# Query rows of the latent layer: 32x32 blocks turned on VectorE and carried by GpSimd in place of transposes on TensorE

## The reference, cut to what matters

```python
u = rms_norm(h, ln) @ w_in                       # -> c_q (512), c_kv (512), k_pe (64), gate (2048)
q = (rms_norm(c_q, ln_q) @ w_q_up).reshape(B, S, 16, 192)
kv = (rms_norm(c_kv, ln_kv) @ w_kv_up).reshape(B, S, 16, 256)
v = kv[..., 128:]
k = concatenate([kv[..., :128], broadcast(k_pe)], axis=-1)
q = rms_norm(q, g_q); k = rms_norm(k, g_k)
q = concatenate([q[..., :128], rope(q[..., 128:], pos)], axis=-1)
k = concatenate([k[..., :128], rope(k[..., 128:], pos)], axis=-1)
o = causal_dense_attention(q, k, v)
return h + (o * silu(gate)) @ w_o
```

## Time and profile before

| | before |
|---|---|
| median of 3 runs | 1396.17 us (1396.0 to 1396.33) |
| profiled execution | 1396.6 us, its span 1394.8 us |
| TensorE busy (matmul) | 1389.4 us |
| VectorE busy | 1040.2 us |
| ScalarE busy | 782.6 us |
| GpSimd busy | 101.5 us |
| granted TensorE clock | 1.00 throughout |

### The profile page before, as it was taken

The page is one execution under the profiler, slowest core; times in us unless marked ns, Lnnn a source line. Parts: engine busy times, 40 slices in busy tenths (PEclk is TensorE's granted clock), DMA queues, the critical chain, the costliest instruction groups (busy, mean ns, idle before and its releaser), DMA issues.

```text
span 1394.8 us, 17859 instructions
## 1 busy us (share of the span) xinstructions
PE 1389.4 (100%) x6584; PEld 1162.1 (83%) x6584; DVE 1040.2 (75%) x1825; ACT 782.6 (56%) x1288; POOL 101.5 (7%) x67
## 2 busy tenths in 40 slices
PE   9999999999999999999999999999999999999999
PEld 6888888888888888888888888888888888888887
DVE  6767767847667868778877886887888688779753
ACT  6577877756544654464465465446545545644642
POOL 0101001000010001010101100101010010001000
PEclk9999999999999999999999999999999999999999
DMA  9653544455556545655654654564556456555554
GB/s 357 228 180 126 163 141 149 148 189 176 184 187 208 184 157 179 206 166 170 192 182 151 208 185 151 191 201 156 176 183 205 155 185 194 163 182 186 167 179 149
DMA packets 71223, 252.40 MB, mean 181 GB/s; under 512 B 7904, under 2 KB 8288, under 8 KB 71136
## 3 DMA queue, kind: packets, MB, share of 16 engines
q1 hardware_dynamic: 70704, 249.95, 54.9%
q10 hardware_dynamic: 432, 1.31, 0.3%
HBM read 249.14 MB, written 2.10 MB: 180 GB/s over the span
## 4 chain that ended last, share of the span: by engine, by line
PE 98%; DMA 1%; DVE 0%; ACT 0%; SPq 0%; POOL 0%; issue 0%
PE acc L1317 90%; PE turn L1349 1%; PE pv_bank L1581 1%; PE score L1566 1%; PE score L1561 1%; PE pv_bank L1585 1%; PE pv_bank L1361 1%; PE score L1457 1%; PE score L1459 1%; DMA raw<-in_w_in 1%; PE og_bank L1369 0%; PE turn L1443 0%; PE pv_bank L1446 0%; PE og_bank L1446 0%; POOL rms L434 0%; PE pv_bank L1340 0%
## 5 line engine op out<-in xcount | busy, mean ns | idle before, releaser
L837 DVE TENSOR_TENSOR w_lo<-raw,w_hi 128x1024 fp32r<-128x1024 f32 x463 | 571.4, 1249 | 196.6 <-ACT w_hi L486 192.7
L486 ACT ACTIVATE w_hi<-raw 128x1024 fp32r<-128x1024 f32 x463 | 482.2, 1050 | 364.0 <-PE acc L1317 355.7
L1317 PE MATMUL acc<-w_hi,xa_hi 128*128 128x512 f32 x956 | 378.6, 396 | 0.3 <-DVE w_lo L837 0.2
L1317 PE MATMUL acc<-w_hi,xa_lo 128*128 128x512 f32 x956 | 373.1, 390 | 0.0
L1317 PE MATMUL acc<-w_lo,xa_hi 128*128 128x512 f32 x956 | 372.5, 390 | 0.0
L1317 PE MATMUL acc<-w_hi,xb_hi 128*128 128x512 f32 (+1 forms) x640 | 249.5, 390 | 0.0
L1317 PE MATMUL acc<-w_hi,xb_lo 128*128 128x512 f32 (+1 forms) x640 | 245.9, 384 | 0.0
L1317 PE MATMUL acc<-w_lo,xb_hi 128*128 128x512 f32 (+1 forms) x640 | 245.6, 384 | 0.0
L1317 PEld LDWEIGHTS acc<-w_hi,xa_lo 128*128 128x128 f32 x956 | 179.4, 188 | 37.9
L1317 PEld LDWEIGHTS acc<-w_hi,xa_hi 128*128 128x128 f32 x956 | 179.7, 188 | 37.4 <-issue 1.1
L1317 PEld LDWEIGHTS acc<-w_lo,xa_hi 128*128 128x128 f32 x956 | 179.7, 188 | 35.6
(11 more groups left out here) (179 smaller groups left out, 1143.9 us busy)
## 6 DMA issues: line engine op xcount, KB each, us to landing
raw<-in_w_b SPq DMA_DIRECT2D x320, 512.0 KB, 3.8
raw<-in_w_out_a SPq DMA_DIRECT2D x32, 512.0 KB, 3.3
raw<-in_w_out_b SPq DMA_DIRECT2D x32, 512.0 KB, 3.3
raw<-in_w_gate SPq DMA_DIRECT2D x30, 512.0 KB, 3.6
raw<-in_w_kv SPq DMA_DIRECT2D x16, 512.0 KB, 3.9
raw<-in_w_in SPq DMA_DIRECT2D x15, 512.0 KB, 6.0
raw<-in_w_q SPq DMA_DIRECT2D x16, 384.0 KB, 3.0
res<-in_x_tok SPq DMA_DIRECT2D x4, 512.0 KB, 8.0
```

The costliest lines, as they stand in the source:

```text
L486: nc.scalar.activation(w[0][:, s, 0:width], raw[:, s, 0:width], ACT.Copy).then_inc(hi_ready, 1)
L837: nc.vector.tensor_tensor(w[1][:, s, 0:width], raw[:, s, 0:width], w[0][:, s, 0:width].bitcast(F32), ALU.subtract).then_inc(lo_ready, 1)
L1317: last = nc.tensor.matmul(out, x(a), y(b), start=start and k == 0, stop=stop and k == 2, **more)
```

## The change

The unrotated query rows take the way that the keys have already: VectorE turns 32x32 blocks of `rows[:, 1]` in place (`mla_query_blocks`) in step 7, after that step's part of the attention and before its `lows`, and GpSimd carries the 16 blocks to `qT` (`query_moves`). ScalarE applies the gain in place in `qT`, in step 2 of the next pair as before, but ahead of its wait for TensorE. TensorE transposes the two rotated tiles alone. ScalarE still carries the keys; of its 16 key moves one goes from step 0 of the next pair to step 3. The last pair does the same within the output projection.

```diff
-KEY_MOVES = {3: range(0, 1), 4: range(1, 4), 7: range(4, 8), 8: range(8, 16)}
+KEY_MOVES = {3: range(0, 2), 4: range(2, 5), 7: range(5, 9), 8: range(9, 16)}
...
+        def nope_rows(buf, span):
+
+            return rows[:, buf, :, 0:2 * span].rearrange("p t (u d) -> p t u d", d=span)[:, :, :, 0:P]
...
+            def query_moves(par):
+
+                queries = nope_rows((MLA_CHAIN_0 + 1) % 2, QK)
+                turned = qT[:, par * 512:(par + 1) * 512].rearrange("p (u t d) -> p t u d", t=TILES, d=P)
+                for n in range(16):
+                    a, b = n // 4, n % 4
+                    last = nc.gpsimd.tensor_copy(turned[b * QUAD:(b + 1) * QUAD, :, :, a * QUAD:(a + 1) * QUAD],
+                                                 queries[a * QUAD:(a + 1) * QUAD, :, :, b * QUAD:(b + 1) * QUAD])
+                last.then_inc(query_turned, 1)
+
             for i in range(0, PAIRS):
-                for s in range(MLA_STEPS):
-                    if s == 1:
-                        chain(i * 2 + MLA_CHAIN_0, 2 * TILES)
-                    if s == 7:
-                        chain(i * 2 + (MLA_CHAIN_0 + 1), 2 * TILES)
+                par = i % 2
+                if i:
+                    pool.wait_ge(query_turned, i)
+                chain(i * 2 + MLA_CHAIN_0, 2 * TILES)
+                chain(i * 2 + (MLA_CHAIN_0 + 1), 2 * TILES)
+                pool.wait_ge(rms_ready, i * 2 + (MLA_CHAIN_0 + 2))
+                pool.wait_ge(query_blocks, i + 1)
+                query_moves(par)
...
-            def mla_queries_turned(par, rnd):
-
+            def mla_queries_turned(i, par, rnd):
+
+                act.wait_ge(query_turned, i)
+                at = qT[:, par * 512:(par + 1) * 512]
+                nc.scalar.activation(at, at, ACT.Copy, scale=gn("q_nope"))
                 act.wait_ge(turn_full, rnd + 1)
-                nc.scalar.activation(qT[:, par * 512:(par + 1) * 512], turn[:], ACT.Copy, scale=gn("q_nope"))
...
                     if s == 5:
+                        if i:
+                            act.wait_ge(query_turned, i)
...
+            def mla_query_blocks(i):
+
+                dve.wait_ge(rows_ready, i * 2 + (MLA_CHAIN_0 + 2))
+                queries = nope_rows((MLA_CHAIN_0 + 1) % 2, QK)
+                nc.vector.transpose(queries, queries).then_inc(query_blocks, 1)
...
                     mla_attend(i, par, s, later, fill)
+                    if s == 7:
+                        mla_query_blocks(i)
...
-            def mla_turn(c, buf, rnd, rope_bank, head_step, rope_0, heads=2):
+            def mla_turn(c, buf, rnd, rope_bank, rope_0):
 
                 pe.wait_ge(rows_ready, c + 1)
                 pe.wait_ge(turn_read, rnd)
-                for h in range(heads):
-                    for t in range(TILES):
-                        nc.tensor.transpose(turn[:, h * SEQ + t * P:h * SEQ + (t + 1) * P],
-                                            rows[:, buf, t, h * head_step:h * head_step + P], ident[:])
```

More of the change, by code:

```diff
@@ L319, in build_program @@
         key_blocks = sem("key_blocks")
+        query_blocks = sem("query_blocks")
+        query_turned = sem("query_turned")
         rot_step = sem("rot_step")
@@ L440, in _ @@
             chain(1, TILES)
-            for i in range(0, PAIRS):
-                for s in range(MLA_STEPS):
-                    if s == 1:
-                        chain(i * 2 + MLA_CHAIN_0, 2 * TILES)
-                    if s == 7:
-                        chain(i * 2 + (MLA_CHAIN_0 + 1), 2 * TILES)
+            def query_moves(par):
[6 more added lines that the diff above has]
+                last.then_inc(query_turned, 1)
+            for i in range(0, PAIRS):
+                par = i % 2
[6 more added lines that the diff above has]
+                query_moves(par)
+            pool.wait_ge(query_turned, PAIRS)
             pool.wait_ge(loaded, 48)
@@ L685, in mla_pair @@
                     if s == 2 and later:
-                        mla_queries_turned(1 - par, mla_round(i, 0))
+                        mla_queries_turned(i, 1 - par, mla_round(i, 0))
                     if s == 3:
@@ L706, in _ @@
                 if k == 4:
-                    mla_queries_turned(1, mla_round(PAIRS, 0))
+                    mla_queries_turned(PAIRS, 1, mla_round(PAIRS, 0))
                 i, _, s = after_pairs(k)
@@ L1161, in mla_pair @@
                     mla_attend(i, par, s, later, fill)
+                    if s == 7:
+                        mla_query_blocks(i)
                     if s == 2:
                         dve.wait_ge(rows_ready, i * 2 + (MLA_CHAIN_0 + 1))
-                        keys = rows[:, MLA_CHAIN_0 % 2, :, 0:2 * P]
+                        keys = nope_rows(MLA_CHAIN_0 % 2, P)
                         nc.vector.transpose(keys, keys).then_inc(key_blocks, 1)
@@ L1208, in _ @@
                     mla_query_rotate(PAIRS - 1)
+                    mla_query_blocks(PAIRS - 1)
                 if k in OUT_FILL_END:
@@ L1483, in mla_queries_turned @@
             def mla_queries_turned(i, par, rnd):
-                mla_turn((i - 1) * 2 + (MLA_CHAIN_0 + 1), (MLA_CHAIN_0 + 1) % 2, rnd, pv_bank, QK, 2 * QK)
+                mla_turn((i - 1) * 2 + (MLA_CHAIN_0 + 1), (MLA_CHAIN_0 + 1) % 2, rnd, pv_bank, 2 * QK)
             def mla_pair(i, par, later, steps=MLA_STEPS):
@@ L1506, in mla_pair @@
                     if s == 3:
-                        mla_turn(i * 2 + MLA_CHAIN_0, MLA_CHAIN_0 % 2, mla_round(i, 1) if later else 4, og_bank, P, 2 * P, 0)
+                        mla_turn(i * 2 + MLA_CHAIN_0, MLA_CHAIN_0 % 2, mla_round(i, 1) if later else 4, og_bank, 2 * P)
             latents = [tuple(x[:, c] for x in lat) for c in range(2)]
```

## The result

The changed kernel takes **1402.16 us** (median of 6 runs, 1401.84 to 1402.57) against 1396.09 us for the kernel before in the same comparison (6 runs): ratio 1.0044, 95% interval 1.0033 to 1.0054. It is 6.1 us slower. The forecast was 1393.2 us, and its chances for "faster" and "within 0.2%" held three quarters; what came is the first rival, "the moves are too slow".

A forecast was written before the change was run, and what follows sets the result against it. TensorE was taken to bound the kernel, with ScalarE's exponential chain last in pairs 2 to 7. 6 x 0.32 + 2 x 0.56 = 3.0 us less gave a 1393.2 us median; 8-in-10 range 1391.5 to 1404 us.

The forecast's parts named there:

- the moves are too slow: Rival: GpSimd's copies overrun and delay the key power and TensorE; 1399.5 us at 0.30 us a move; chance 0.35.
- What bounds the kernel now: TensorE sets the time, but in pairs 2 to 7 waits 0.30 us each for ScalarE's exponential, whose chain ends last.
- I take 0.20 us: Assumed time of one GpSimd query move, 3.2 us for a pair's sixteen, leaving 0.5 us to spare.
- The limit of 0.234 us a move: Most a GpSimd move may take before the key power is late: 3.74 us of free time for 16 moves.
- The low halves: VectorE's low halves at 196.05 to 197.25 and 197.75 to 198.7 keep GpSimd's copies out for their whole length.
- The overshoot o: Time by which GpSimd's moves run past 201.94, when the key power is wanted; sum 6 x (0.32 - o) + 1.1 us.
- The four transposes, 0.56 us a pair,: TensorE's saving from four transposes less in each pair, 4.5 us over eight pairs if TensorE alone set the time.
- The chain gives 0.32 us in pairs 2 to 7: One key move less in ScalarE's step 0 shortens the chain to the exponential by 0.32 us a pair.
- The whole 0.56 us: Full transpose saving claimed for the first turned queries (pair 1) and the last (output projection).
- The covers: Idle time or slack was to hide VectorE's 0.70 us block turn, later loads, ScalarE's 0.32 us step 3 move and gain.
- The moves shut VectorE out: Rival: sixteen GpSimd copies in a row hold the shared access and delay VectorE's low halves; 1398 us; chance 0.07.
- The chain gives way: Rival: TensorE's wait at 207.98 has more slack, so the full 4.5 us come out; 1391.7 us; chance 0.08.

The follow-up runs named there:

- e5: Changed kernel with GpSimd's key power between the twelfth move and the last four, and ScalarE copying the rotated parts ahead of the gain: 1405.92 us.
- e7: Changed kernel with VectorE's block turn of the queries behind the low half of step 7, the last pair unaltered: 1404.33 us.
- e6: Changed kernel with ScalarE copying the two rotated parts ahead of the gain, not behind it: 1401.85 us.
- e8: Changed kernel with 12 query moves on GpSimd, four on ScalarE, and the last pair's block turn one output projection step later: 1394.71 us.
- e11: Changed kernel with only the last pair's block turn one step later in the output projection: 1402.47 us.
- e9: Changed kernel with TensorE's four transposes of the query rows put back, into a bank nobody reads: 1402.45 us.
- e2: Changed kernel with GpSimd carrying only 12 or 4 of 16 query blocks, the others left out: 1395.81 us and 1394.72 us.
- e10: Changed kernel with GpSimd carrying all key blocks and ten query blocks, ScalarE six, the last block turn one step later: 1395.97 us.

## Why the prediction was wrong, step by step

- **What bounds the kernel now** held. TensorE's wait for the exponential was the place, and it took the loss of the changed kernel in pairs 2 to 7 and the small gain with 12 or 4 moves. The further losses of e5 and e7 show at the scores, behind the gain, a path that the prediction named only as a cover.
- **The step that failed is the term "I take 0.20 us" for a GpSimd move.** It was worked out from 128-partition fills, which read nothing. Measured are 0.29 us for a copy and 0.33 us from start to start, so 16 x 0.328 = 5.25 us in place of 3.2: 2.05 us more against a margin of 0.5 us. That a copy follows the one before closely held (0.04 us); what was too small is the copy itself, for which the text's lower bound had 0.115 us. The limit of 0.234 us a move was strict but fair (the runs put it at (5.89 - 0.14 - 1.50) / 16 = 0.266); the taken value had no row of a copy behind it. The nearest row in kind, ScalarE's 0.32 us for the same 32x128 block, was in the text, as an example inside the rival, and it was right. The estimate that the text made by the Trainium skill (GPSIMD Engine Reference, on performance against the Vector engine and on pitfalls), 0.28 us a move, was nearer than mine as well: the copy took 0.29, but its start to start took 0.33.
- **The low halves** were counted too dear. They took 0.83 and 0.67 us from the copies (1.12 and 0.96 less the usual 0.29), 1.50 in place of 2.15 us: each of the two copies began 0.22 and 0.13 us into its low half, and part of its own 0.29 us ran beside. With the 0.14 us between block turn and first copy the power starts 5.25 + 1.50 + 0.14 = 6.9 us after the block turn; 5.89 were free. The overshoot o is 1.0 us, and 6 x (0.32 - 1.0) = -4.1 us; measured were -3.9. The direction of the exclusion was right and its size fair.
- **The four transposes, 0.56 us a pair,** were mis-sized. Before, the six loads from 201.44 to the next `acc` at 202.21 took 0.77 us; now two take 0.34 us (204.63 to 204.97). The saving is 0.43 us. I had read it off the starts of two groups, and the first group's start-up stays with whatever group is first.
- **"The chain gives 0.32 us in pairs 2 to 7"** could only be seen with the overshoot taken away: with 12 or 4 moves the pairs are 26.76 us against 27.02 to 27.03, so 0.27 us. TensorE's wait there is 0.45 us, which is 0.30 + 0.43 - 0.27; 0.54 was forecast. So this half of the forecast was the right mechanism and a bit large.
- **"The whole 0.56 us" for the first and the last** was wrong both times, and for reasons that had rows. In pair 1 no unit's store stands ahead of the sums, so the key means come sooner after the block turn: they are done at 93.40 us, the copies at 95.35, and the power starts at 95.43. TensorE, which had not waited in this pair, waits 1.3 us for the exponential, and 0.48 and 0.22 us on the way there; e6, without the 0.48, loses as much in this pair. In the last pair the block turn has `og` and TensorE close behind it: 0.87 us, shown by e8. With sixteen copies it can't be had back, since the scores wait instead (e11).
- **The covers** held where they were claimed: the block turn in pairs 1 to 7 costs nothing (VectorE's idle time fell from 2.89 to 2.17 us), and no wait of TensorE in pairs 2 to 7 points at the move in step 3 or at the later loads. The gain on ScalarE did wait for GpSimd (12.8 us in all). That cost nothing where the scores had slack; in pair 1 they had none and TensorE waited 0.48 us, which e6 shows to be covered by the wait for the power.
- **The rivals.** "Too slow" came, with its formula nearly right for the wrong reason: at 0.33 us a move it gives o = 1.5 and 1402.2 us, the measured time, but a true o of 1.0 is made up for by the two losses at the ends that it priced as gains. That its time agrees is luck. "The moves shut VectorE out" did not come: both low halves kept their length in this pair, and the longest beside copies, in e10, took 1.34 us. "The chain gives way" fell with e9 and e2: more than 0.27 us a pair is not there.

## What to carry to other kernels

When work goes to an engine that already has one small job on a critical chain, ask when that job is wanted and how long the new work holds it. Here 16 copies behind 5.9 us of room cost 6 us in all; 12 of them, with 4 on ScalarE, gained 0.9, and 1.5 with the last block turn moved as well. Price a small instruction by a row of the same kind and shape on another engine before you take one from a different operation on the same engine. And where a loop is in order by hand, price its first and last pass apart, since their neighbours differ.

## What the runs showed of the hardware that was not expected

- A GpSimd copy of 32 partitions x 128 f32 takes 0.283 to 0.29 us undisturbed, 0.33 us from start to start, about what ScalarE takes (2.22 us for seven, 0.32 each). A fill of four times the elements on 128 partitions took 0.46 us from start to start.
- In the exclusion with VectorE's low halves the later one loses, and with short copies that is cheap for VectorE. A copy that starts after a low half has begun stands still to its end (1.12 and 0.96 us), while the low half lasts 1.18 and 0.95 us, as without copies. A low half that starts while a copy runs loses at most the rest of that copy. With 0.10 us of the copy left it keeps its length (200.66); with 0.27 us left it takes 1.34 us, up from 1.22 (VectorE in e10):

```profile
186.17 1.34 DVE L879 TENSOR_TENSOR w_lo<-raw,w_hi 128x1024 fp32r<-128x1024 f32 x1 [1.62 <-ACT w_hi L521]
```

The next copy then stands still in its turn (1.19 us). In the earlier trace rows one long GpSimd instruction had made a low half take 3603 ns. So a row of short instructions lets VectorE in after each, and pays for it itself. The Trainium skill (SBUF - State Buffer, on who interferes with whom) says that the two exclude each other for the whole instruction; the trace agrees for the copies.
- Of a run of six transposes, taking four away saved 0.43 us in the loads, and putting four back took 0.32 us off the wait (e9, pairs 2 to 7). Why the two differ by 0.1 us stays open.
